# Convolution up stages: twelve of 22 feature pairs as seven block products

## The reference

```
def conv_ffn(h, w_up, conv_w, conv_b, w_down):
    u = h @ w_up                                   # 1024 -> 2 x 2816
    up = jnp.pad(u, ((0, 0), (CONV_WIDTH - 1, 0), (0, 0)))
    conv = conv_b
    for j in range(CONV_WIDTH):                    # three taps along the tokens
        conv = conv + conv_w[j] * up[:, j:j + s]
    a, g = jnp.split(conv, 2, axis=-1)
    return (jax.nn.silu(a) * g) @ w_down
```

## Time and profile before

| | |
|---|---|
| median of 3 runs | 2323.34 us (2322.82 to 2324.22) |
| span of the profiled execution | 2320.9 us |
| its own time beside the span | not given apart from the span; the median lies 2.4 us above it |
| TensorE busy | 2309.1 us, 99% |
| VectorE busy | 1498.3 us, 65% |
| ScalarE busy | 1119.0 us, 48% |
| GpSimd busy | 223.6 us, 10% |
| granted TensorE clock | 1.00 throughout |

### The profile page before, as it was taken

One profiled execution on the slowest core, in us unless ns is written; L12 is line 12 of the kernel. 1 busy time (PEld: TensorE's weight loads), 2 busy tenths in 40 slices (PEclk: granted clock), 3 DMA queues, 4 the chain that ended last, 5 costly groups with the idle time before them and its releaser, 6 DMA issues.

```text
span 2320.9 us, 32131 instructions
## 1 busy us (share of the span) xinstructions
PE 2309.1 (99%) x12088; PEld 1950.9 (84%) x12088; DVE 1498.3 (65%) x2173; ACT 1119.0 (48%) x1829; POOL 223.6 (10%) x313
## 2 busy tenths in 40 slices
PE   9999999999999999999999999999999999999999
PEld 8777889988888888999888778888888878888887
DVE  6665789952738968899428876777434456777731
ACT  6655544452539965445326854444323444544420
POOL 1221013200125410232000000000001000000000
PEclk9999999999999999999999999999999999999999
DMA  5433223332242222333322223323322323233232
GB/s 167 152 132 102 85 92 109 104 112 93 87 118 64 64 84 82 99 110 111 113 89 77 64 82 91 100 90 106 100 93 91 100 69 95 91 100 100 95 107 79
DMA packets 72541, 226.30 MB, mean 98 GB/s; under 512 B 7921, under 2 KB 19489, under 8 KB 72417
## 3 DMA queue, kind: packets, MB, share of 16 engines
q1 hardware_dynamic: 67840, 210.72, 28.5%
q0 software_dynamic: 4576, 13.89, 1.9%
HBM read 221.28 MB, written 2.18 MB: 96 GB/s over the span
## 4 chain that ended last, share of the span: by engine, by line
PE 92%; DVE 3%; ACT 3%; POOL 1%; issue 1%; DMA 0%; DVEq 0%; ACTq 0%; SPq 0%
PE bank L338 26%; PE bank L340 25%; PE bank L339 25%; PE bank L478 5%; PE bank L470 4%; PE bank L1605 1%; PE bank L1596 1%; PE bank L1639 1%; DVE w_lo L312 0%; DVE h L756 0%; POOL hgrn_lv L2560 0%; PE bank L2651 0%; PE bank L2015 0%; POOL hgrn_lv L2547 0%; PE bank L3103 0%
## 5 line engine op out<-in xcount | busy, mean ns | idle before, releaser
L312 DVE TENSOR_TENSOR w_lo<-raw,w_hi 128x1024 fp32r<-128x1024 f32 (+1 forms) x310 | 402.3, 1308 | 218.4 <-ACT w_hi L307 218.1
L338 PE MATMUL bank<-x_hi,w_hi 128*128 128x512 f32 x1344 | 529.2, 394 | 1.2 <-ACT sb_q L2761 1.0
L340 PE MATMUL bank<-x_hi,w_lo 128*128 128x512 f32 x1344 | 523.4, 389 | 0.0
L339 PE MATMUL bank<-x_lo,w_hi 128*128 128x512 f32 x1344 | 523.1, 389 | 0.0
L307 ACT ACTIVATE w_hi<-raw 128x1024 fp32r<-128x1024 f32 (+1 forms) x310 | 344.6, 1121 | 179.9 <-PE bank L340 93.5
L338 PEld LDWEIGHTS bank<-x_hi,w_hi 128*128 128x128 f32 x1344 | 252.3, 188 | 57.4 <-issue 3.1
L340 PEld LDWEIGHTS bank<-x_hi,w_lo 128*128 128x128 f32 x1344 | 252.2, 188 | 53.0
L339 PEld LDWEIGHTS bank<-x_lo,w_hi 128*128 128x128 f32 x1344 | 252.5, 188 | 51.2 <-issue 0.5
L338 PE MATMUL bank<-st_a_hi,w_hi 128*128 128x512 f32 (+1 forms) x396 | 145.1, 366 | 0.0
L340 PE MATMUL bank<-st_a_hi,w_lo 128*128 128x512 f32 (+1 forms) x396 | 144.7, 365 | 0.0
L1374 DVE TENSOR_TENSOR bank<-bank,rstd 128x512 f32<-128x512 f32 x120 | 83.2, 696 | 92.2 <-PE bank L340 92.2
(11 more groups left out here) (444 smaller groups left out, 4673.2 us busy)
## 6 DMA issues: line engine op xcount, KB each, us to landing
raw<-in_w_up SPq DMA_DIRECT2D x120, 512.0 KB, 3.5
raw<-in_w_down SPq DMA_DIRECT2D x64, 704.0 KB, 4.2
st_raw_even<-in_w_up SPq DMA_DIRECT2D x28, 512.0 KB, 4.2
st_raw_odd<-in_w_up SPq DMA_DIRECT2D x24, 512.0 KB, 4.0
raw<-in_w_fox_qk SPq DMA_DIRECT2D x16, 512.0 KB, 3.7
raw<-in_w_hgrn_qf SPq DMA_DIRECT2D x16, 512.0 KB, 3.5
fox_c_keys_a<-fox_c_rows POOLq DMA_DIRECT2D x8, 640.0 KB, 4.1
fox_c_keys_b<-fox_c_rows POOLq DMA_DIRECT2D x8, 640.0 KB, 4.5
```

The costliest lines, as they stand in the source:

```text
L312: nc.vector.tensor_tensor(w_lo[:, slot, 0:size], raw[:, slot % 2, 0:size], w_hi[:, slot, 0:size].bitcast(F32), ALU.subtract).then_inc(sem( ...
L338: nc.tensor.matmul(out, w[0], x[0], start=first, stop=False)
L339: nc.tensor.matmul(out, w[0], x[1], start=False, stop=False)
L340: return nc.tensor.matmul(out, w[1], x[0], start=False, stop=last)
```

## The change

In up2 and up3 the first ten pairs stay plain (CV_FIRST = 10), and twelve are made as seven block products. Unlike in up0, products are added up in PSUM: products 0, 2, 4 and 6 of a pair go one after the other onto the same half bank, and ScalarE copies the bank out between them (`cv_first`, `cv_second`). Product 3 and then product 5 go to the second half of another bank, product 1 to its first half. The order of the products over the pairs is `CV_ORDER`: in round k products 2 and 1 of pair k, 6 of pair k - 1, 3 of pair k, 0 of pair k + 1, 4 and 5 of pair k. VectorE puts together three of the four result blocks (`c1`, `c22`), ScalarE the fourth (`c21`). The result goes to SBUF (`st_out`), and all taps read it there. The input forms are made in VectorE's and ScalarE's programs of pairs 2 to 7, and pair 0's weight sums are split in those of the last two plain pairs.

The low part of weight block 6 is not made by VectorE: after the high part ScalarE writes the same rounded block negated (scale -1) in its place, and a DMA of GpSimd's queue adds the raw block from DRAM to it (256 KB). It adds one ScalarE instruction of 512 elements and one DMA per pair, and removes one VectorE instruction.

`up_a_hi` and `up_a_lo` are gone. The high and low parts of all 22 hidden tiles are made at the end of the stage, as in up0, and the first two down units are taken tile by tile in all four stages. SP loads down unit 0 once `cv_minus_g` allows, and down unit 1 once all twelve `cv_c22` are counted. Parts of the diff:

```diff
+        CV_FIRST = 10
+        CV_PAIRS = FT - CV_FIRST
...
+        def cv_sum_bank(n):
+            return ps[(6, 7, 3)[n % 3]][:, HALVES[0]]
+        def cv_row_bank(n):
+            return ps[4 + n % 2]
+        def cv_order():
+            order = [(0, 0)]
+            for k in range(CV_PAIRS):
+                order += [(k, 2), (k, 1)]
+                if k:
+                    order.append((k - 1, 6))
+                order.append((k, 3))
+                if k < CV_PAIRS - 1:
+                    order.append((k + 1, 0))
+                order += [(k, 4), (k, 5)]
+            return order + [(CV_PAIRS - 1, 6)]
+        CV_ORDER = cv_order()
...
+        def cv_pe(pe, f, n, i):
+            g = CV_PAIRS * (f - 2) + n
+            a, first = cv_sum_bank(n), i in (0, 1, 3)
+            if i == 0:
+                if n == 0:
+                    wait(pe, "cv_xlo", 7 * (f - 2) + 7)
+                if n == 2:
+                    pe.wait_ge(sem("gated_ready"), FT * f + CV_FIRST + 2)
+                if n >= 3:
+                    wait(pe, "cv_c21", g - 2)
+                wait(pe, "cv_lo_a", g + 1)
+            elif i == 2:
+                wait(pe, "cv_first", g + 1)
+                wait(pe, "cv_lo_s12", g + 1)
+            elif i == 6:
+                wait(pe, "cv_c22", g + 1)
+                wait(pe, f"cv_added{g % 2}", 16 * (g // 2) + 16)
+            elif i == 1:
+                if n >= 2:
+                    wait(pe, "cv_c1", g - 1)
+            elif i == 4:
+                wait(pe, "cv_second", g + 1)
+                wait(pe, "cv_lo_s3", g + 1)
+            elif i == 5:
+                wait(pe, "cv_m5", g + 1)
+                wait(pe, "cv_lo_s4", g + 1)
+            out = {1: cv_row_bank(n)[:, HALVES[0]], 3: cv_row_bank(n)[:, HALVES[1]], 5: cv_row_bank(n)[:, HALVES[1]]}.get(i, a)
+            for k in range(QUAD):
+                w = [st_w(n, h, slice(i, i + 1))[:, 0, k * P:(k + 1) * P] for h in range(2)]
+                ins = mm3(out, w, [cv_form_hi[i][:, k, :], cv_form_lo[i][:, k, :]], first and not k, k == QUAD - 1, True)
+            if i == 6:
+                ins.then_inc(sem("unit_used"), 2)
+            else:
+                ins.then_inc(sem("cv_part"), 1)
...
+            src, at = cv_block(n, blocks)
+            nc.scalar.activation(st_w(n, 0, at), src, ACT.Copy).then_inc(sem("cv_hi_" + blocks), 1)
+            if blocks == "g":
+                nc.scalar.activation(st_w(n, 1, at), src, ACT.Copy, scale=-1.0).then_inc(sem("cv_minus_g"), 1)
...
+        def cv_act_copy(act, f, n, step):
+            cv_done(act, f, n, 2 * step)
+            nc.scalar.activation(cv_pu[n % 2][:, step, :], cv_sum_bank(n), ACT.Copy).then_inc(
+                sem("cv_second" if step else "cv_first"), 1)
+        def cv_act_c21(act, f, n):
+            cv_done(act, f, n, 6)
+            nc.scalar.activation(st_out[:, 2, :], cv_sum_bank(n), ACT.Copy, scale=-1.0).then_inc(sem("cv_c21"), 1)
+        def cv_act_m5(act, f, n):
+            cv_done(act, f, n, 3)
+            if n:
+                wait(act, "cv_c22", CV_PAIRS * (f - 2) + n)
+            nc.scalar.activation(cv_minus5[:], cv_row_bank(n)[:, HALVES[1]], ACT.Copy, scale=-1.0).then_inc(sem("cv_m5"), 1)
...
+        def cv_act_a_hi(act, f, ks):
+            for k in ks:
+                if k < 20 and k % 4 == 0:
+                    cv_done(act, f, CV_PAIRS - 1, (0, 2, 1, 3, 4)[k // 4])
+                elif k == 20:
+                    cv_done(act, f, CV_PAIRS - 1, 5)
+                act.wait_ge(sem("gated_ready"), FT * f + k + 1 + 2)
+                nc.scalar.activation(a_early[:, k, :], a_plain(k), ACT.Copy).then_inc(sem("ahi_ready"), 1)
+        def act_conv(act, f):
+            last = CV_PAIRS - 1
+            down = following[f"up{f}"]
+            cv_act_copy(act, f, 0, 0)
+            cv_act_hi(act, f, 1, "a")
+            for k in range(CV_PAIRS):
+                if k:
+                    cv_act_tap(act, f, k - 1, 0)
+                cv_act_copy(act, f, k, 1)
+                if k < last:
+                    cv_act_hi(act, f, k + 1, "s12")
+                if k:
+                    cv_act_c21(act, f, k - 1)
+                    cv_act_tap(act, f, k - 1, 1)
+                cv_act_m5(act, f, k)
+                if k:
+                    cv_act_silu(act, f, k - 1)
+                if k < last:
+                    cv_act_hi(act, f, k + 1, "s3")
+                if k < last:
+                    cv_act_copy(act, f, k + 1, 0)
+                    cv_act_hi(act, f, k + 1, "g")
+                    cv_act_hi(act, f, k + 1, "s4")
+                if k < last - 1:
+                    cv_act_hi(act, f, k + 2, "a")
+            act.sem_inc(sem("hi_ready"), 2 * CV_PAIRS)
+            convert_act(act, 0, down.first, down.size)
+            cv_act_a_hi(act, f, range(0, 10))
+            convert_act(act, 1, down.first + 1, down.size)
+            cv_act_a_hi(act, f, range(10, 16))
+            cv_act_tap(act, f, last, 0)
+            cv_act_c21(act, f, last)
+            cv_act_tap(act, f, last, 1)
+            cv_act_a_hi(act, f, range(16, 18))
+            cv_act_silu(act, f, last)
+            cv_act_a_hi(act, f, range(18, FT))
...
+                wait(pool, "cv_minus_g", g + 1)
+                unit = io[f"w_up{f}"][2 * (CV_FIRST + n) + 1].rearrange("p (b x) -> p b x", b=2)
+                pool.dma_start(st_w(n, 1, slice(6, 7)), unit[:, 1:2, :], accum_op=ALU.add).then_inc(sem(f"cv_added{g % 2}"), 16)
...
+        def cv_dve_c1(dve, f, n):
+            g = CV_PAIRS * (f - 2) + n
+            cv_done(dve, f, n, 5)
+            wait(dve, "cv_first", g + 1)
+            wait(dve, "cv_second", g + 1)
+            nc.vector.tensor_tensor(st_out[:, 0:2, :], cv_pu[n % 2][:], cv_row_bank(n)[:].rearrange("p (b x) -> p b x", b=2),
+                                    ALU.add).then_inc(sem("cv_c1"), 1)
+        def cv_dve_c22(dve, f, n):
+            cv_done(dve, f, n, 4)
+            wait(dve, "cv_m5", CV_PAIRS * (f - 2) + n + 1)
+            if n:
+                dve.wait_ge(sem("conv_ready"), 2 * (FT * (f - 2) + CV_FIRST + n))
+            nc.vector.tensor_tensor(st_out[:, 3, :], cv_minus5[:], cv_sum_bank(n), ALU.subtract).then_inc(sem("cv_c22"), 1)
...
+        def dve_conv(dve, f):
+            last = CV_PAIRS - 1
+            down = following[f"up{f}"]
+            for k in range(CV_PAIRS):
+                if k:
+                    cv_dve_c1(dve, f, k - 1)
+                if k < last:
+                    cv_dve_lo(dve, f, k + 1, "a")
+                    cv_dve_sum(dve, f, k + 1, False)
+                if k:
+                    cv_dve_taps(dve, f, k - 1, 0)
+                if k < last:
+                    cv_dve_lo(dve, f, k + 1, "s12")
+                    cv_dve_sum(dve, f, k + 1, True)
+                if k:
+                    cv_dve_taps(dve, f, k - 1, 1)
+                if k < last:
+                    cv_dve_lo(dve, f, k + 1, "s3")
+                if k:
+                    cv_dve_gate(dve, f, k - 1)
+                if k < last:
+                    cv_dve_lo(dve, f, k + 1, "s4")
+                    cv_dve_c22(dve, f, k)
+            dve.sem_inc(sem("split_ready"), 2 * CV_PAIRS)
+            convert_dve(dve, 0, down.first, down.size)
+            cv_dve_a_lo(dve, f, range(0, 6))
+            cv_dve_c22(dve, f, last)
+            cv_dve_c1(dve, f, last)
+            cv_dve_a_lo(dve, f, range(6, 8))
+            cv_dve_taps(dve, f, last, 0)
+            convert_dve(dve, 1, down.first + 1, down.size)
+            cv_dve_taps(dve, f, last, 1)
+            cv_dve_a_lo(dve, f, range(8, 12))
+            cv_dve_gate(dve, f, last)
+            cv_dve_a_lo(dve, f, range(12, FT))
...
+                if name in ("down2", "down3"):
+                    f = int(name[4])
+                    for i in range(2):
+                        st_raw_wait(sp, f, CV_PAIRS - 1, i)
+                    wait(sp, "cv_lo_s4", CV_PAIRS * (f - 2) + CV_PAIRS - 1)
+                    for i in range(2):
+                        wait(sp, ("cv_minus_g", "cv_c22")[i], CV_PAIRS * (f - 2) + CV_PAIRS - 1 + i)
```

More of the change, by code:

```diff
@@ L223, in build @@
         ps = [ctx.enter_context(nc.psum_tensor(f"bank{i}", [P, T], F32)) for i in range(8)]
-        up = Region("up")
-        a_hi = up.take("a_hi", [P, FT, T], F32R)
-        a_lo = up.take("a_lo", [P, FT, T], F32R)
-        conv_g = up.take("conv_g", [P, T])
         A_MAIN = 17
@@ L334, in used, with mm3 @@
             pe_or_other.wait_ge(sem("unit_used"), u + 1 + CREDIT)
-        def mm3(out, w, x, first, last):
-            nc.tensor.matmul(out, w[0], x[0], start=first, stop=False)
-            nc.tensor.matmul(out, w[0], x[1], start=False, stop=False)
-            return nc.tensor.matmul(out, w[1], x[0], start=False, stop=last)
+        def mm3(out, w, x, first, last, onto=False):
+            nc.tensor.matmul(out, w[0], x[0], start=first, stop=False, skip_group_check=onto)
```

(54 more changed lines are left out.)

243 lines of the change are left out of this document (188 added, 55 removed).

## The result

The changed kernel takes 2398.94 us, the median of 4 runs (2398.09 to 2399.15), the kernel before in the same series 2323.66: a ratio of 1.0325, 95% interval 1.031 to 1.034. The profiled execution has a span of 2397.3 us, 76.4 more than before. Forecast were 2343.0 us with a range up to 2362: the sign was right and the size far off.

The account below looks back on a forecast made before the run. TensorE, busy 99%, was taken as the bound. Per stage -9.6 + 1.95 + 4.3 + 5.15 + 7.7 + 0.3 = +9.8, two stages +19.7 us, giving 2343.0 us; range 2332 to 2362.

Parts of the forecast that it names:

- Spared: TensorE in the twelve pairs: 10.08 us a pair instead of 10.88, 9.6 us less per stage.
- Preparation: Pairs 2 to 9: VectorE's some 22 us of new work fits its free time, cost 0 (ends 0 and 2).
- The 6.2 us of cover: Pairs 2 to 9: time between a bank's normal freeing and its next use, covering VectorE's lag of about 5 us.
- The first wait: Pair 0 of the twelve: product 2 waits for ScalarE's copy `cv_first`, 1.95 us per stage (ends 1.5 and 2.5).
- The loop: Twelve pairs: VectorE needs 10.7 us a pair against TensorE's 10.08; seven pairs wait, 4.3 us per stage.
- Rival 1: Loop: both GpSimd additions meet VectorE's SBUF work, 11.6 us a pair, 6.6 us more per stage, 2356 us; chance 0.18.
- 2.5 us in hand: Start of the loop: TensorE's slack, as product 6 wants `c22` only third in the next round; used up after two pairs.
- The last product 6: Stage end: product 6 of pair 11 waits for VectorE's `c22`, 5.15 us per stage (ends 4.5 and 6).
- Tile 8: Down unit 0 after the stage: TensorE waits for `a_lo` of tile 8, 7.7 us per stage (ends 6 and 9).
- The clock: TensorE's granted clock in the two long waits: forecast at no cost; a fall was left to rival 3.
- rival 3: The clock falls to 1.2 GHz in the two long waits at the end, 3.5 us more per stage, 2350 us; chance 0.21.

Follow-up runs that it names:

- The filler kernel: Unused 256-column matmuls (60, 40 and 50 per stage) while TensorE waits, added to the changed kernel: 2392.0 us, 1.030 of the kernel before.

## Why the prediction was wrong, by its steps

- **Spared, -9.6 a stage: right.** A pair costs TensorE 10.08 us where nothing holds it, as taken from up0.
- **Preparation, 0 (0 to 2): wrong.** The step that failed is "about 3.5 us free in each of eight pairs". The time is free, but VectorE passes it waiting in `convert_dve` for ScalarE, with the preparation queued behind. The 6.2 us of cover were reckoned for the banks; the earlier of the two waits here, of 2.5 us, came for `w_lo`, which they don't cover. Undoing it is worth 14.5 us, 7.2 a stage: waits of 4.7 or 3.1, and the slow matmuls behind them (clock 0.76 and 0.90 in the windows from 1485).
- **The first wait, 1.95 (1.5 to 2.5): wrong.** "The scaling starts 0.2 us after TensorE's last matmul" is true of a plain pair; here the weight preparation of pair 0, which an earlier step of the same text had counted, stands ahead of that scaling in VectorE's order, and pair 1's additions meet it. Measured were 8.15 and 9.4 us. GpSimd's additions made 3.0 and 4.4 of that (both additions on VectorE), the order most of the rest: with the preparation out of the way 2.5 and 3.1 us were measured.
- **The loop, 10.7 a round: own work right, contention wrong.** 9.23 against 9.26. The text took 0.3 + 1.1 for the two additions, with one hidden by `c22` and `c1`. Both come before these, one behind the other, and hold one VectorE instruction through both: 2.6. Rival 1 had the place (11.6 forecast, 11.83 measured). It is also paid more often: seven pairs were to wait, since TensorE had 2.5 us in hand, but it waits in ten rounds of up2 and nine of up3, 15.4 and 14.6 us where rival 1 had 10.9 (its own 7 x 1.52 is 10.6).
- **The last product 6, 5.15: exact,** in both stages, and by the order of work that was given for it: with `c22` first the wait is gone.
- **Tile 8, 7.7: mechanism right, too large.** From `c22` to tile 8 are 14.8 us (14.6 forecast), but TensorE took 9.9 us (up2) and 8.5 (up3) instead of 6.9 to reach it, at the lower clock.
- **The clock, 0 in the forecast, 3.5 a stage in rival 3.** The sum of the forecast put nothing for it. The filler kernel gives 6.9 us for both stages: the rival's size is right.
- **The sum.** Rivals 1 and 3 both came true, and together they would have given 2363 (2343 + 2 x 6.6 + 2 x 3.5), already outside a range that treated them as apart. Of the 36 us beyond, the preparation is 14.5 and the first wait 13.7, both in large part from VectorE's order of work, which the text had weighed as sums of free time; the loop is 8 us over rival 1.

## What to carry to other kernels

Free time of an in-order engine is worth only what stands ready in its queue when it gets free: list the queue, not the sum, and put work without inputs ahead of instructions that wait. Work given to GpSimd beside a VectorE that is nearly full is not free, and can cost more than doing it on VectorE; if it waits for something, ask what it then meets. Where two rivals have the same root, a TensorE that waits, price them together.
